# Four norms between products: the pieces beside them taken by token tile, the norms by halves

## What is computed

```
def first_block(x, ...):
    mix = hybrid_mixer(x, ...)                       # w_in, SSD and GLA heads, two branches, gates, w_out
    x = layer_norm(ALPHA * x + mix, ln1_g, ln1_b)
    x = layer_norm(ALPHA * x + squared_relu_mlp(x, w_up, w_down), ln2_g, ln2_b)

def _layer(x, g_pre, g_post, w_in, ..., w_out):      # twice
    h = _rms_norm(x, g_pre)
    proj = h @ w_in                                  # then three kinds of attention heads
    y = concat(o_a, o_b, o_c) @ w_out
    return x + _rms_norm(y, g_post)
```

## Time and profile before

| | us |
|---|---|
| runs, median of 3 | 3055.98 (3054.32 to 3056.18) |
| profiled execution | 3052.53 |
| its span | 3051.1 |
| TensorE busy in it | 2929.7 (96%), 13611 matmuls and transposes |
| DVE busy | 1773.5 (58%) |
| ACT busy | 1481.4 (49%) |
| granted TensorE clock, mean | 0.976 of full |

### The profile page before, as it was taken

The page is one execution under the profiler, slowest core; times in us unless marked ns, Lnnn a source line. Parts: engine busy times, 40 slices in busy tenths (PEclk is TensorE's granted clock), DMA queues, the critical chain, the costliest instruction groups (busy, mean ns, idle before and its releaser), DMA issues.

```text
span 3051.1 us, 34750 instructions
## 1 busy us (share of the span) xinstructions
PE 2929.7 (96%) x13611; PEld 2430.2 (80%) x13611; DVE 1773.5 (58%) x2261; ACT 1481.4 (49%) x2033; POOL 0.4 (0%) x5
## 2 busy tenths in 40 slices
PE   8999999999999999998999999996999997999997
PEld 7888888888887788786888888885887776887776
DVE  4556766666655565655655555554566446566545
ACT  4456666666555554444433434343444434444444
POOL 0000000000000000000000000000000000000000
PEclk8999999999999999998999999998999998999999
DMA  6767676766766677764665656654666665666664
GB/s 207 223 206 235 224 231 227 239 229 228 243 222 227 216 243 269 263 201 154 198 193 172 207 179 199 187 184 141 209 212 194 198 198 200 199 214 192 197 211 152
DMA packets 347138, 634.99 MB, mean 208 GB/s; under 512 B 36557, under 2 KB 58317, under 8 KB 344414
## 3 DMA queue, kind: packets, MB, share of 16 engines
q1 hardware_dynamic: 268736, 506.13, 51.6%
q10 hardware_dynamic: 78238, 126.64, 12.3%
HBM read 582.99 MB, written 49.69 MB: 207 GB/s over the span
## 4 chain that ended last, share of the span: by engine, by line
PE 88%; DVE 4%; DMA 4%; ACT 2%; ACTq 2%; issue 1%; DVEq 0%
PE bank L893 27%; PE bank L895 26%; PE bank L894 26%; PE bank L548 2%; PE bank L761 1%; DMA arena<-in_sin 1%; DVE w_lo L1535 1%; PE bank L777 1%; DMA raw<-in_w_gla_branch 1%; PE bank L613 1%; ACTq L1394 1%; DMA raw<-in_w_out 1%; ACT w_hi L921 1%; PE bank L750 1%; DMA arena<-in_norm_pre 0%
## 5 line engine op out<-in xcount | busy, mean ns | idle before, releaser
L1535 DVE TENSOR_TENSOR w_lo<-raw,w_hi 128x1024 fp32r<-128x1024 f32 (+2 forms) x980 | 1158.6, 1206 | 738.6 <-ACT w_hi L921 728.8
L893 PE MATMUL bank<-w_lo,x_hi 128*128 128x512 f32 (+2 forms) x3920 | 1547.1, 395 | 23.9 <-DVE stage L2017 13.1
L895 PE MATMUL bank<-w_hi,x_lo 128*128 128x512 f32 (+2 forms) x3920 | 1526.4, 389 | 0.0
L894 PE MATMUL bank<-w_hi,x_hi 128*128 128x512 f32 (+2 forms) x3920 | 1526.1, 389 | 0.0
L921 ACT ACTIVATE w_hi<-raw 128x1024 fp32r<-128x1024 f32 (+2 forms) x980 | 992.9, 1044 | 732.2 <-PE bank L895 273.8
L893 PEld LDWEIGHTS bank<-w_lo,x_hi 128*128 128x128 f32 x3920 | 745.1, 190 | 178.7 <-DVE stage L2017 15.3
L895 PEld LDWEIGHTS bank<-w_hi,x_lo 128*128 128x128 f32 x3920 | 744.6, 190 | 152.0
L894 PEld LDWEIGHTS bank<-w_hi,x_hi 128*128 128x128 f32 x3920 | 745.4, 190 | 147.8 <-issue 2.9
L926 ACT ACTIVATE x_hi<-bank 128x512 fp32r<-128x512 f32 (+1 forms) x120 | 67.0, 590 | 311.9 <-PE bank L548 311.9
L1540 DVE TENSOR_TENSOR x_lo<-bank,x_hi 128x512 fp32r<-128x512 f32 (+1 forms) x120 | 78.2, 679 | 194.4 <-ACT x_hi L926 194.0
L548 PE MATMUL bank<-ident,arena 128*128 128x128 f32 x472 | 74.7, 310 | 72.6 <-DVE arena L1829 48.2
(11 more groups left out here) (190 smaller groups left out, 1114.0 us busy)
## 6 DMA issues: line engine op xcount, KB each, us to landing
raw<-in_w_in SPq DMA_DIRECT2D x496, 512.0 KB, 4.8
raw<-in_w_up SPq DMA_DIRECT2D x128, 512.0 KB, 3.8
raw<-in_w_down SPq DMA_DIRECT2D x128, 512.0 KB, 4.6
raw<-in_w_out SPq DMA_DIRECT2D x96, 512.0 KB, 4.7
raw<-in_w_ssd_branch SPq DMA_DIRECT2D x64, 512.0 KB, 5.8
proj<-stage ACTq DMA_DIRECT2D x60, 512.0 KB, 5.2
arena<-proj ACTq DMA_DIRECT2D x50, 512.0 KB, 5.0
raw<-in_w_gla_branch SPq DMA_DIRECT2D x32, 512.0 KB, 5.2
```

Of the source, the lines that this page charges most:

```text
L893: pe.matmul(o, x_hi[:, xk, tokens(t)], w_lo[:, r, k, 0:b.n], start=a, stop=False)
L894: pe.matmul(o, x_hi[:, xk, tokens(t)], w_hi[:, r, k, 0:b.n], start=False, stop=False)
L895: op = pe.matmul(o, x_lo[:, xk, tokens(t)], w_hi[:, r, k, 0:b.n], start=False, stop=z_)
L1535: TT(w_lo[:, p % SPLIT_RING, 0:b.per, 0:b.n], raw[:, p % RAW_RING, 0:b.per, 0:b.n], w_hi[:, p % SPLIT_RING, 0:b.per, 0:b.n].bitcast(F32), ...
```

## The change

The list of pieces is walked by TensorE in another order around the four norms: the last four pieces before it (`HALVED`) are done for token tile 0, then for tile 1, and so are the first four pieces behind it. With two pieces in a block of `rest`, the last four are those of the last two blocks, and each of these two is drained by halves.

The stages `layer_norm`, `pre_norm` and `post_norm` go; one side stage, `edge`, takes their place. It begins at the last piece of the product and is spread by its `yield`s over the first pieces of the next. Sums, statistics and root are made per token tile. The eight chunks of 512 columns and one tile are taken in the order of `CHUNKS` (column block, tile), and TensorE transposes each at a fixed place among its pieces and waits only for the x_lo that the next two pieces need. For `layer_norm`, `bn_stats` at each drain and `bn_aggr` take the place of the copies with read-out, the shift and the squares. For `pre_norm`, only the gain is multiplied in before the product; squares and root (`hs`) come later, on ACT at the fourth piece behind, and the factor is applied at the drains of the attention products (`scaled`, `out_of_bank`). Its gain is loaded at `sum_begins` 1 (layer 0) and in `post_begins` (layer 1). An early root on a spare cell brings ACT's table. The output of the last norm is stored in eight parts instead of two. `skew`, `sum_begins` 1 and `post_begins` begin at other pieces.

```diff
+CHUNKS = ((0, 0), (1, 0), (0, 1), (1, 1), (2, 0), (2, 1), (3, 0), (3, 1))
+HALVED = 4
+HN_RING = 3
...
+def in_turn(blocks):
+    order, group = [], []
+    def close():
+        order.extend((b, q, (t,)) for t in range(NT) for b, q in group)
+        group.clear()
+    last = None
+    for b in blocks:
+        for q in range(b.pieces):
+            name = b.halved.get(q)
+            if group and name != last:
+                close()
+            last = name
+            if name is None:
+                order.append((b, q, tuple(range(NT))))
+            else:
+                group.append((b, q))
+    close()
+    return order
...
+    def edge_of(n, last):
+        left = HALVED
+        for b in reversed(last):
+            b.own = n
+            for q in range(b.pieces - 1, -1, -1):
+                if left:
+                    b.halved[q] = ("end", n)
+                    left -= 1
+        sides.append((b.last if b is last[-1] else last[-1].last, "edge", (n,)))
+        if n < 3:
+            last[-1].turns[last[-1].pieces - 1, 1] = (n, 0)
+    def edge_into(n, b):
+        for q in range(HALVED):
+            b.halved[q] = ("begin", n)
+        for m, at in enumerate(((0, 0), (3, 0), (0, 1), (2, 1), (3, 1), (4, None), (5, None))):
+            b.turns[at] = (n, m + 1)
...
-    b.flush = True
-    b.after = [("layer_norm", 0)]
+    edge_of(0, [b])
 
     w_down = i["w_down"][0]
     for f in range(FF // D):
         for j in range(NB):
             b = block(weight_at(i["w_up"][0], f * D + j * BLK, BLK), 0, KT, BLK, "hidden", f, j)
             if f == 0 and j == 0:
-                beside(b, "sum_begins", 1)
+                edge_into(0, b)
+                beside(b, "sum_begins", 1, at=12)
...
-        b.before = [("pre_norm", l)]
+        edge_into(1 + l, b)
         begin = b.first
-        beside(b, "skew", l, at=1)
+        beside(b, "skew", l, at=10)
...
-                b.before = [("post_begins", l)]
-        b.flush = True
-        b.after = [("post_norm", l)]
+                beside(b, "post_begins", l, at=0)
+        edge_of(2 + l, blocks[-2:])
+    blocks[-1].ends = True
...
+        def turn_chunk(n, m):
+            c, t = CHUNKS[m]
+            if m >= 4:
+                pe.wait_ge(*edge.dve["lo", n, m - 4])
+            pe.wait_ge(*edge.dve["chunk", n, m])
+            source = total[:, t, c * BLK:(c + 1) * BLK] if n == 0 else hns[n - 1][:, m % HN_RING, :]
+            turn(4 + m % 4, source).then_inc(*edge.pe("turned", n, m))
...
+            begins = b.halved.get(0, ("", 0))
+            if begins[0] == "begin" and q % 2 == 0:
+                pe.wait_ge(*edge.dve["lo", begins[1], CHUNKS.index((k, ts[-1]))])
...
+            for b, q, ts in in_turn(blocks):
+                p = b.first + q
+                r = p % SPLIT_RING
+                turned_now = b.turns.get((q, ts[0] if len(ts) == 1 else None))
+                if turned_now:
+                    turn_chunk(*turned_now)
+                if q == 0 and ts[0] == 0:
+                    for name, *info in b.before:
+                        for _ in stages[name](*info):
+                            pass
+                    if b.number >= 2:
+                        pe.wait_ge(*drained_by(blocks[b.number - 2]))
...
+                if ts[-1] == 0:
+                    if q == b.pieces - 1:
+                        op.then_inc(*tail(b.number))
+                    continue
+                op.then_inc(*summed(p))
...
+            if n == 1:
+                act.dma_start(pre_gs[0], row_of(i["norm_pre_2"][0], D)).then_inc(*load[2]("pre", 0))
...
+            def squares(t):
+                l = n - 2
+                for j in (NB - 2, NB - 1):
+                    act.wait_ge(*edge.dve["sum", n, j, t])
+                    act.wait_ge(*post.act.now)
+                    A(junk[:, t * BLK:(t + 1) * BLK], total[:, t, j * BLK:(j + 1) * BLK], ACT.Square,
+                      accum_out=sq2[:, t, j:j + 1]).then_inc(*post.act("square", l, j, t))
+            def take(m):
+                c, t = CHUNKS[m]
+                act.wait_ge(*edge.pe["turned", n, m])
+                high(4 + m % 4, 4 * c, t).then_inc(*edge.act("hi", n, m))
+            def send(t, chunk):
+                act.wait_ge(*edge.dve["y", n, chunk])
+                act.dma_start(rows(out[0])[:, t, :], total[:, t, :]).then_inc(*out_done(n - 1, t))
+            def one_over_root(t):
+                root_of(edge, (n, t), mean_var[:, t, 1:2] if n < 2 else root[:, t, :])
             if n:
-                for t in range(NT):
-                    act.wait_ge(*norm.dve["y", n, t, KT - 4])
-                    act.dma_start(rows(out[0])[:, t, :], total[:, t, :]).then_inc(*out_done(0, t))
-            yield
-
-        def pre_norm(l):
-            if l == 0:
-                act.wait_ge(*norm.dve["y", 1, NT - 1, KT - 4])
-            else:
-                act.wait_ge(*post.dve["out", l - 1, NT - 1])
-            act.dma_start(pre_g, row_of(i["norm_pre_2"][l], D)).then_inc(*load[1]("pre", l))
-            for t in range(NT):
-                A(hn[:, t, :], total[:, t, :], ACT.Square, accum_out=ssq[:, t, :]).then_inc(*pre.act("square", l, t))
-            act.wait_ge(*summed[start_of["latent_in", 1, l].first - 1])
-            for t in range(NT):
-                root_of(pre, (l, t), ssq[:, t, :])
-                for m in range(4 * t, 4 * t + 4):
-                    act.wait_ge(*pre.pe["turned", l, m])
-                    high(4 + m % 4, 4 * (m % 4), t).then_inc(*pre.act("hi", l, m))
-            yield
+                act.wait_ge(*edge.act.now)
+            A(spare, ident[:, 0:1], ACT.Sqrt).then_inc(*edge.act("ready", n))
+            if n >= 2:
+                squares(0)
+            one_over_root(0)
+            if n < 3:
+                take(0)
+            if n >= 2:
+                squares(1)
+            one_over_root(1)
+            if n == 3:
+                for m, (c, t) in enumerate(CHUNKS):
+                    act.wait_ge(*edge.dve["y", n, m])
+                    cols = slice(c * BLK, (c + 1) * BLK)
+                    act.dma_start(rows(out[0])[:, t, cols], total[:, t, cols]).then_inc(*out_done(n - 1, m))
+                return
+            take(1)
+            take(2)
+            take(3)
+            yield 1
+            take(4)
+            take(5)
+            yield 2
+            take(6)
+            take(7)
+            if n:
+                yield 3
+                send(0, 6)
+                send(1, 7)
+                yield 4
+                for t in range(NT):
+                    if t:
+                        act.wait_ge(*edge.act.now)
+                    A(junk, total[:, t, :], ACT.Square, accum_out=hs[:, t, :]).then_inc(*edge.act("square", n, t))
+                yield 5
+                root_of(edge, (n, "hs"), flat(hs))
...
-            act.dma_start(xr, rows(out[0])).then_inc(*load[1]("post", l))
             act.dma_start(post_g, row_of(i["norm_post_2"][l], D)).then_inc(*load[1]("post", l))
+            if l + 1 < LAYERS:
+                act.dma_start(pre_gs[l + 1], row_of(i["norm_pre_2"][l + 1], D)).then_inc(*load[2]("pre", l + 1))
+            act.dma_start(xr, rows(out[0])).then_inc(*load[0]("xr", l))
...
+        def scaled(b):
+            if b.kind == "latent_in" or b.info[0] == "proj2":
+                act.wait_ge(*edge.act["root", 1 + b.info[-1], "hs"])
+                return {"scale": hs[:, 0, :]}
+            return {}
...
+        def edge_stage(n):
+            ends = [b for b in blocks if b.own == n]
+            def sums(t):
+                for b in ends:
+                    what, j, _ = b.info
+                    dve.wait_ge(*(summed[b.last] if t else tail[b.number]))
+                    dve.wait_ge(*drain_dve.now)
+                    some = total[:, t, j * BLK:(j + 1) * BLK]
+                    TT(some, bank[2 * b.half + t][:, :], some, ALU.add).then_inc(*edge.dve("sum", n, j, t))
+                dve.wait_ge(*edge.dve.now)
+                if n < 2:
+                    dve.bn_stats(stats[:, t, 6 * (NB - 1):], some).then_inc(*edge.dve("stats", n, t))
+                    dve.wait_ge(*edge.dve.now)
+                    dve.bn_aggr(mean_var[:, t, :], stats[:, t, :]).then_inc(*edge.dve("mean", n, t))
+                    dve.wait_ge(*edge.dve.now)
+                    r = mean_var[:, t, 1:2]
+                    root_of(edge, (n, t), r, r, 1, 1e-5)
+                else:
+                    for j in (NB - 2, NB - 1):
+                        times_gain(n - 2, j, (t,))
+                    dve.tensor_reduce(root[:, t, :], sq2[:, t, :], AX, ALU.add).then_inc(*edge.dve("squares", n, t))
+                    dve.wait_ge(*edge.dve.now)
+                    root_of(edge, (n, t), root[:, t, :], root[:, t, :], D, 1e-6)
+                    dve.wait_ge(*post.dve.now)
+                dve.wait_ge(*edge.act["root", n, t])
+            def chunk(m):
+                c, t = CHUNKS[m]
```

(68 more changed lines are left out.)

232 lines of the change are left out of this document (61 added, 171 removed).

## The result

The changed kernel takes 3020.81 us in the median of four runs (3018.26 to 3025.62), the kernel before 3055.15 beside it (3054.29 to 3056.18): a recorded ratio of 0.9893, 95% interval 0.9878 to 0.9909 (the two medians alone give 0.9888). Forecast were 3019.7 us and 3008 to 3034. A second set of four runs gave 3020.83 and 0.9896 (0.9880 to 0.9913). The profiled execution took 3020.04 (span 3018.6).

A forecast was written before the change was run, and what follows sets the result against it. TensorE, busy 96%, bounds the kernel; its idle time at four edges can be won: 12.0 + 14.5 + 6.8 + 3.0 = 36.3 us, so 3016.2 for the profiled execution and 3019.7 for the median, range 3008 to 3034.

The forecast's parts named there:

- A: Edge at the first layer norm: tile 0's norm runs beside TensorE's matmuls on tile 1; gain 12.0 us.
- the clock: Lower TensorE clock after long waits: each wait of 2.5 us or more costs 1.7 us, partly absorbed.
- B: Edge at the second layer norm and first pre-norm: DVE is the bound, waits total 13.1 us; gain 14.5 us.
- the squares: Attention norm's two squares on ACT, ahead of the next block's weight conversion: 2.9 us lost in B and in C.
- C: Edge at layer 0's post-norm and layer 1's pre-norm: DVE comes late; gain 6.8 us, ends 0 and 11.
- the MB: At C, norm_pre adds 1 MB to ACT's queue, so the w_out piece waits 2.8 us more.
- D: Last post-norm and output: output begins 3.2 us earlier, in eight stores; gain 3.0 us, ends 0 and 4.5.
- Elsewhere: Outside the edges: changed copies, drains, norm-vector loads and skew, all hidden by TensorE; 0 to 2 us of loss.
- the low clock that holds: Rival: the half-rate clock holds through the edges' matmuls, 81 us more, 3101 us; chance 0.04.
- The late stores at B and C: Rival: the weights' queue starves behind 2 MB stores, costing 4.1 us at each edge, 3028 us; chance 0.17.
- The longer queue: Rival: DVE's queue is longer, bn_stats at 1.2 and later hand-overs; gain 22.5 us, 3033.5 us; chance 0.17.
- The sign of idle time over 45 us: Sign that the forecast is wrong: the edges' idle time stays above 45 us in sum.

## Why the prediction was right, step by step

**A.** The statistics instructions were priced at 0.69 and 0.25 and took 0.69 and 0.26. The waits 0.7, 3.1 (at 23.0) and 0.9 became 0.53, 3.05 (at 23.2) and 0.75. The one term well off in the first profile is the clock: 0.8 us was allowed, 2.8 were lost. Over eight profiles the loss is 0.5 in the mean, six times nothing; the second profile's gain is 12.4 for 12.0. The allowance was right as a mean and could not have been right for one execution.

**B.** Forecast 14.5, measured 14.4 and 15.2. VectorE gives chunks too slowly, as worked out, so there are many small waits; chunk 5 waits 1.31 for 2.1, chunk 6 3.65 for 3.6, the next block 1.61 for 2.9. The last is the squares, over-priced by half; laid apart they cost nothing. That the sum came out is in part luck. Up to the block behind, the forecast has 16.0 us of waits and 24.6 of work and clock, 40.6; the first profile has 11.7 and 29.0, 40.7. The granted clock over this stretch is 0.87, which costs 5.1 us at most, where 1.8 were allowed. C, counted from the first half piece on, has the same pair of errors: 18.6 and 29.1 forecast, 12.2 and 35.7 measured.

**C.** Forecast 6.8, measured 6.8 twice. The wait ahead of the half pieces came as forecast (4 to 5, 4.34), for the reason given (2.4 us for the MB, 2.8 forecast), and chunk 0, x_lo 1 and chunk 6 wait 3.14, 2.14 and 2.87 for 3.5, 2.6 and 2.9. Here too 1.3 of the squares' 2.9 did not come.

**D.** 3.0 forecast. What lies behind the product gave 2.9 (13.9 to 11.0). The other 2.3 in the first profile are the wait ahead of the first half piece, 2.48 and here 1.62, and a half clock after it that did not come; the second profile has 3.5. This wait ran from 1.62 to 3.32 in executions whose code there was alike.

**Elsewhere.** "0 to 2 us of loss, hidden by TensorE", counted as 0, was the step that failed, by 3.5 and 2.8 us in the two profiles, and by 6.4 when their mean is compared with the mean of three profiles of before. The drains with a factor, the loads and the table were looked at one by one for their own time and not for what they do to the units, where VectorE stands on a landing and a drain stands behind it. Part of it is seen: the first unit's wait is 1.34 to 1.87 in the six cases of before, and 1.90 to 3.99 in sixteen of the changed kernel and of edits elsewhere. It follows the last load, in_sin: asked for 11 to 13 us ahead of the wait in all of them, it lands 6.9 to 9.1 us after it was asked for in before (mean 7.9) and 7.8 to 10.1 in the others (mean 8.8). Why it takes longer was not settled; the place of the bias table, which moved with the change, is not enough to explain it. The time came out within 1.1 us of the forecast by luck: the profiled execution is 3.8 above the 3016.2 of the sum, but the median of before stood 3.45 above its profiled execution and the changed kernel's only 0.8.

Of the rivals, the low clock that holds (3101) did not come: stretches of four microseconds at 0.50 are there in A in the first profile (1394 to 1398) and in B (2122 to 2126), and over the whole of A, B and C the granted clock is 0.91, 0.87 and 0.91 in the first profile and 1.00, 0.87 and 0.91 in the second. The late stores at B and C (3028) did not either; the block behind waits for the squares and not for weights. The longer queue (3033.5) fell with the 0.69 of the statistics. The sign of idle time over 45 us was close: from "0" on, the waits of A, B and C and what lies behind the product in D sum to 39.2 in both profiles, and to 45.1 and 45.4 with the waits ahead of the half pieces in C and D.

## What to carry to other kernels

A product that ends in a norm can be taken by token tile over its last few pieces: the gain is the time of the other tile's matmuls, almost whole, as long as the vector engine is not already late (6 us a place in A and B, 2.9 in C). Then look at what stands in each engine's queue ahead of the chunk that comes late; one chunk moved ahead of two conversions, two squares laid apart, one load asked for later and four stores sooner were worth 14 us together, and they added up. Price a half clock after a wait of 3 us as a chance, and take more than one profile of the kernel before: the time to the first edge scattered by 4.5 us over its three profiles, and the part from C to D by 3.0. Last, what is left out of a sum as "hidden" should be looked at by what it does to loads and drains; here it was the one term that failed.
